# Reordering the feed-forward units that follow a two-step unit: turns, high parts and low parts

## The reference

```python
def _swiglu(x, w_gate, w_up, w_down):
    return (jax.nn.silu(x @ w_gate) * (x @ w_up)) @ w_down
```

## Time and profile before

| | us |
|---|---|
| median of the runs | 1314.61 |
| the profiled execution, its own time | 1314.64 |
| its span on the core | 1312.8 |
| PE matmul busy | 1298.3 (99%) |
| PE weight load busy | 1109.5 (85%) |
| DVE busy | 1080.2 (82%) |
| ACT busy | 791.2 (60%) |
| POOL busy | 140.0 (11%) |

### The profile page before, as it was taken

How to read it: one execution, slowest core, us unless ns; L and a number is a source line. 1 busy time by engine, 2 the same in 40 slices (tenths; PEclk the granted TensorE clock), 3 DMA queues, 4 the chain that set the end, 5 groups by cost and what they waited for, 6 DMA issues and landing times.

```text
span 1312.8 us, 19267 instructions
## 1 busy us (share of the span) xinstructions
PE 1298.3 (99%) x7299; PEld 1109.5 (85%) x7300; DVE 1080.2 (82%) x1306; ACT 791.2 (60%) x1038; POOL 140.0 (11%) x212
## 2 busy tenths in 40 slices
PE   9999999999999999999999999999999999999997
PEld 6978999998878889977888888878889988887886
DVE  6977876677999874577999979999876988999985
ACT  6674655555666645585576655666646854566661
POOL 5420000000000100183000000000000001100000
PEclk9999999999999999999999999999999999999999
DMA  9535766665698766515689868598755434779860
GB/s 318 170 107 167 241 192 192 190 206 216 204 319 271 199 222 207 188 24 193 209 257 282 271 204 299 161 326 281 201 184 181 158 100 153 285 214 310 279 183 33
DMA packets 160785, 275.53 MB, mean 210 GB/s; under 512 B 7297, under 2 KB 105874, under 8 KB 156610
## 3 DMA queue, kind: packets, MB, share of 16 engines
q1 hardware_dynamic: 150512, 226.51, 50.0%
q0 software_dynamic: 9904, 46.85, 16.0%
q10 hardware_dynamic: 290, 1.11, 0.2%
HBM read 238.24 MB, written 1.07 MB: 182 GB/s over the span
## 4 chain that ended last, share of the span: by engine, by line
PE 92%; DVE 5%; issue 2%; ACT 1%; DVEq 0%; POOL 0%; ACTq 0%
PE ps L912 18%; PE ps L914 18%; PE ps L913 18%; PE ps L734 6%; PE ps L736 6%; PE ps L735 6%; PE ps L935 3%; PE ps L936 2%; PE ps L942 2%; DVE wlo L681 2%; PE ps L3157 1%; PE ps L1922 1%; PE ps L1095 1%; PE ps L1902 1%; PE ps L1936 1%
## 5 line engine op out<-in xcount | busy, mean ns | idle before, releaser
L642 DVE TENSOR_TENSOR wlo<-raw,whi 128x1024 fp32r<-128x1024 f32 x230 | 273.7, 1224 | 45.6 <-ACT whi L632 44.4
L670 ACT ACTIVATE whi<-arena 128x2048 fp32r<-128x2048 f32 x112 | 214.6, 1916 | 98.4 <-PE ps L914 95.8
L632 ACT ACTIVATE whi<-raw 128x1024 fp32r<-128x1024 f32 x230 | 232.2, 1053 | 63.5 <-PE ps L914 45.7
L681 DVE TENSOR_TENSOR wlo<-arena,whi 128x2048 fp32r<-128x2048 f32 x112 | 255.8, 2287 | 13.8 <-ACT whi L670 12.8
L912 PE MATMUL ps<-whi,ahi 128*128 128x512 f32 x456 | 180.7, 396 | 0.0
L914 PE MATMUL ps<-wlo,ahi 128*128 128x512 f32 x456 | 177.7, 390 | 0.0
L913 PE MATMUL ps<-whi,alo 128*128 128x512 f32 x456 | 177.7, 390 | 0.0
L734 PE MATMUL ps<-ahi,whi 128*128 128x256 f32 x624 | 177.2, 284 | 0.0
L736 PE MATMUL ps<-ahi,wlo 128*128 128x256 f32 x624 | 176.6, 283 | 0.0
L735 PE MATMUL ps<-alo,whi 128*128 128x256 f32 x624 | 176.6, 283 | 0.0
L734 PEld LDWEIGHTS ps<-ahi,whi 128*128 128x128 f32 x624 | 119.7, 192 | 0.9 <-issue 0.3
(11 more groups left out here) (457 smaller groups left out, 2404.4 us busy)
## 6 DMA issues: line engine op xcount, KB each, us to landing
raw<-ffn_w_down SPq DMA_DIRECT2D x88, 512.0 KB, 10.0
arena<-ffn_w_gate SPq DMA_DIRECT2D x32, 1024.0 KB, 8.5
arena<-ffn_w_up SPq DMA_DIRECT2D x32, 1024.0 KB, 8.1
arena<-arena POOLq DMA_DIRECT2D x32, 1024.0 KB, 7.8
raw<-w_up SPq DMA_DIRECT2D x44, 512.0 KB, 4.6
raw<-ffn_w_gate SPq DMA_DIRECT2D x24, 512.0 KB, 4.7
raw<-ffn_w_up SPq DMA_DIRECT2D x24, 512.0 KB, 6.0
raw<-w_down SPq DMA_DIRECT2D x22, 512.0 KB, 4.1
```

What stands on the lines that cost most here:

```text
L632: act.activation(split_half(w_slots(slot)[0], mode), raw_half(h), ACT.Copy).then_inc(hi_ready, 1)
L642: dve.tensor_tensor(lo, raw_half(h), hi.bitcast(F32), ALU.subtract).then_inc(lo_ready, 1)
L670: act.activation(hi, src, ACT.Copy).then_inc(hi_ready, 2)
L681: dve.tensor_tensor(lo, src, hi.bitcast(F32), ALU.subtract).then_inc(lo_ready, 2)
```

## The change

In a unit behind a two-step unit:

- PE: t1 comes ahead of the turn of step 1, and the turn of step 2 comes behind b22. The order is b11, b21, t1, turn 1, t2, b22, turn 2, t3, down step 1, down step 2, t4.
- ACT: the high part of b22 and the snapshot v5 come ahead of the high part of turn 1; the high part of turn 2 comes behind the high part of t3 and the snapshot v_u2. As t1 no longer stands behind the second gated product on PE, v5 now waits for it (`gated_ready`).
- DVE: the low part of turn 1 comes behind the low part of b22, and that of turn 2 behind the low part of down step 1.

In a two-step unit that is followed by a two-step unit, also where it follows a single one, DVE writes the low part of the following t1 ahead of the second gated product.

The diff:

```diff
--- before.py
+++ after.py
@@ -1160,15 +1160,15 @@
                     product("b11", block(0, 0), z, True, True)
                     pe.wait_ge(silu_ready, done + FFN_STEPS + 2)
                     product("b21", block(0, 1), r, True, True)
+                    product("t1", block_sum(1), 1, True, True)
                     pe.wait_ge(gated_ready, done + 2)
                     turn(pair_step(before, 0), range(NT))
-                    product("t1", block_sum(1), 1, True, True)
-                    pe.wait_ge(g_ready, turns + before.steps[0] + 1)
-                    turn(pair_step(before, 1), range(NT))
                     pe.wait_ge(snap_ready, 3 * d + 1)
                     product("t2", block_sum(2), z, False, True)
                     pe.wait_ge(snap_ready, 3 * d + 2)
                     product("b22", block_sum(4), 1, False, True)
+                    pe.wait_ge(g_ready, turns + before.steps[0] + 1)
+                    turn(pair_step(before, 1), range(NT))
                     pe.wait_ge(snap_ready, 3 * d + 3)
                     product("t3", block_sum(3), z, False, True)
                 else:
@@ -1318,16 +1318,18 @@
 
                 def snap_y():
                     act.wait_ge(half_done, g.at["t1"] + 2)
+                    if before.double:
+                        act.wait_ge(gated_ready, mult_count(n) + 2 * i)
                     act.activation(v5, ps[:, 1, :], ACT.Copy).then_inc(snap_ready, 1)
 
                 if before.double:
                     act_block(act, n, c + 3)
-                    turned((0, 1), turns + before.steps[0] + 1)
                     act_block(act, n, c + 4)
                     snap_y()
-                    turned((0, 1), turns + before.steps[1] + 1, last_ghi)
+                    turned((0, 1), turns + before.steps[0] + 1)
                     act_block(act, n, c + 5)
                     snap_z()
+                    turned((0, 1), turns + before.steps[1] + 1, last_ghi)
                 else:
                     turned((0, 1), turns + before.steps[0] + 1)
                     act_block(act, n, c + 3)
@@ -1442,20 +1444,19 @@
                 g, c = parts[i], place_of(n, parts[i].at["b11"])
                 before, following, downs = parts[i - 1], parts[i + 1], len(g.downs)
                 d, z, r = g.d, ps[:, g.first, :], ps[:, 2 - g.first, :]
-                if before.double:
-                    dve_block(dve, n, c + 3)
+                if not before.double:
                     turned((0, 1), turns + before.steps[0] + 1)
-                else:
-                    turned((0, 1), turns + before.steps[0] + 1)
-                    dve_block(dve, n, c + 3)
+                dve_block(dve, n, c + 3)
                 dve.wait_ge(snap_ready, 3 * d + 1)
                 dve.wait_ge(half_done, g.at["b21"] + 2)
                 dve.tensor_tensor(g.v1, r, g.v1, ALU.add).then_inc(c_ready, 1)
                 dve_block(dve, n, c + 4)
                 if before.double:
-                    turned((0, 1), turns + before.steps[1] + 1, last_ghi, last_glo)
+                    turned((0, 1), turns + before.steps[0] + 1)
                 dve_block(dve, n, c + 5)
                 dve_block(dve, n, c + 6)
+                if before.double:
+                    turned((0, 1), turns + before.steps[1] + 1, last_ghi, last_glo)
                 dve.wait_ge(half_done, g.at["t3"] + 2)
                 dve.wait_ge(snap_ready, 3 * d + 3)
                 dve.tensor_tensor(v5, v5, z, ALU.subtract).then_inc(c_ready, 1)
@@ -1474,10 +1475,13 @@
                 dve_block(dve, n, c + 8 + downs)
                 if following.double and not before.double:
                     dve_t(dve, following, 2)
+                if following.double:
+                    dve_block(dve, n, c + 9 + downs)
                 dve.wait_ge(silu_ready, silus + 2 * i + 2)
                 dve.wait_ge(c_ready, 2 * d + 2)
                 dve.tensor_tensor(g1, g1, v5, ALU.mult).then_inc(gated_ready, 1)
-                dve_block(dve, n, c + 9 + downs)
+                if not following.double:
+                    dve_block(dve, n, c + 9 + downs)
 
             product(0, 0)
             dve.wait_ge(x_copied, 5 * f + 4)
```

## The result

The changed kernel takes 1332.2 us (median of four runs, 1331.85 to 1332.86); the kernel before took 1314.68 beside it (1314.24 to 1315.19). The ratio is 1.0132, 95% interval 1.012 to 1.0145: slower, by 17.5 us in the medians. A second set of runs gave 1332.01 against 1315.15, again 1.0132 (1.0117 to 1.0148). The forecast was 1330.2, with a range of 1323 to 1335.

The account below looks back on a forecast made before the run. PE, busy 99% of the span, bounds the kernel, with DVE near its limit. Each stage loses 0.79 us, then 1.55 in each of two loops, 3.89; four stages add 15.6 to 1314.64, giving 1330.2 us, range 1323 to 1335.

Parts of the forecast that it names:

- Part 1: Low part of t1 ahead of the second gated product on DVE: 0.15 us won once per stage, in the first unit.
- Part 2: Turn 2 behind b22: ACT's halves for down step 1 come late, PE stalls 0.94 us in each of twelve units.
- E: The end of b22 on PE, from which the forecast counts the times of later starts in a unit.
- the four terms: DVE's delay to down step 1's low parts: turn 0.63, copy 0.49, silu 0.52, first half to low part 1.09; sum 2.73.
- The cover: Before the change, down step 1's first low part was ready 1.8 us ahead of PE's need; nothing replaces that.
- Part 3: DVE's list is too full to catch up after its idle time, so the following b21 is late; 1.55 us lost per loop.
- the loop: Time from one unit to the next within a stage: 32.46 us against 30.91, the 0.94 stall included.
- The sum: Down step 1 late by 0.79, 2.34 and 3.89 us in a stage's three units; four stages 15.6 us, 1330.2 us.
- Only the down step late: Rival, chance 0.12: DVE catches up between the units, so PE stalls only at down step 1; 1325.3 us.
- The reordering hides everything: Rival, chance 0.04: the whole wait for t1 goes, 1.17 us in each stage, 4.7 us faster; 1309.9 us.
- the change does nothing: Rival, chance 0.06: t1 still waits on DVE, 0.6 us won, the down halves lose nothing; 1314.0 us.
- The clock falls: Rival, chance 0.02: PE's stalls lower its clock for one product in each of 12 units, 27 us on top; 1358 us.

Follow-up runs that it names:

- experiment 1: Changed kernel, but ACT writes the high parts of down step 1 ahead of turn 2's high part; 1314.93 us, ratio 0.9997.
- Experiment 4: Changed kernel, but ACT applies silu to v1 behind the high parts of down step 1 instead of ahead of them; 1325.28 us, ratio 1.0077.
- experiment 10: Kernel before, PE's order unchanged; only turn 2's high part on ACT and low part on DVE moved as in the changed kernel; 1315.13 us, ratio 0.9996.
- experiment 5: The changed kernel measured again, unaltered; 1332.01 us, ratio 1.0132.
- experiments 6 and 7: DVE forms the sum n2 over 64 of 2048 columns only: in the changed kernel 1322.56 us, in the kernel before 1310.4 us.
- experiment 9: Kernel of experiment 1, DVE making both gated products behind t1's low part, PE's wait for the first ahead of b11 removed; 1317.13 us, ratio 1.0013.
- experiment 7: Kernel before, with DVE's sum n2 formed over 64 of 2048 columns only; 1310.4 us, ratio 0.9965.
- experiment 8: Kernel of experiment 1, with the first gated product of each two-step unit made by POOL in place of DVE; 1316.18 us, ratio 1.0007.

## Why the prediction was right

*Part 1.* t1 was to start at 368.52; it starts at 368.53, the offset taken off. It was to win 0.15 per stage, and down step 1 of the first unit is 0.80 late, as 0.94 - 0.15 says. As a gain of its own it came out smaller: in the profile of experiment 1, where nothing else is late, the four stages win 0.06, 0.10, 0.11 and 0.09, and in the times that can't be told from nothing. The mis-sized term is the turn: its transposes take 0.35 and the product behind them 2.85 in place of 2.72 (by starts, 377.44 to 377.79 to 380.64 in the first stage of experiment 1), so it costs 0.48 and not 0.45, and 0.60 less 0.48 is 0.12; in the first stage t1 takes 0.04 longer besides.

*Part 2.* DVE at E + 2.73 came out exactly, put together from four rows of other places, and each of the four terms is there within 0.01 (0.64, 0.49, 0.52, 1.08). There are twelve waits of 0.73 to 0.74 idle, where 0.94 less 0.16 was due. Down step 1 at E + 4.11 came at E + 4.10, but here two errors met. The forecast's 0.16 for a wait of PE, taken from the wait for t1, is 0.05 until PE starts and 0.11 that the first matmuls lose behind the start. At down step 1 PE starts 0.15 behind the end of the first half's low part (381.53 + 1.23 = 382.76, and 382.90), and the loss behind the start comes on top: down step 1 lasts 5.54 (382.90 to 388.44), where it lasts 5.44 before. So the price of this wait is 0.25, and that the start itself fell on the forecast's time is luck. Experiment 4 shows that the steps of that sum act one for one, experiment 10 that the turn must be late as well. The cover that the forecast named, 1.8 us, was all the cover there was.

*Part 3.* b21 at E + 21.07 came at E + 21.05, eight times with 0.34 to 0.37 idle, and the loop is 32.51 to 32.54 where 32.46 was due. The stretch from b21 to the next turn 2 is 11.46 (399.85 to 411.31) instead of 11.39, and the difference is again the price of a wait: b21 starts 0.15 behind the end of its low part and then takes 2.80 instead of 2.72, 0.23 in all, where the forecast had 0.16. Eight loops at 0.06 more make 0.5 us.

*The sum.* The starts of down step 1 in the first stage are late by 0.80, 2.40 and 4.03, the 1.48 taken off, where 0.79, 2.34 and 3.89 were forecast. The four stages come to 16.1 us where 15.6 were forecast. The single unit behind, which was to keep 3.89, has another 0.12 in each stage (its down steps are at +5.64, those of the third unit start at +5.52), together 0.5. It does not arise there: it is what down step 1 of the third unit loses behind its own start (447.95 to 453.52, 5.57 us). In the first two units the same loss disappears in the wait for b21. So the change costs 16.6 us by the trace, and the whole 1.0 that the forecast lacks is the price of a wait of PE, 0.23 to 0.25 in place of 0.16. The span grew by 18.2; the remaining 1.5 lie ahead of 354 us and are not the change's, and in the profile of experiment 5 the same count is 16.6 of a growth of 17.0. Against the medians, 17.5 and 16.9, 0.9 and 0.3 stay unassigned.

*The rivals.* Only the down step late: wrong, there are eight waits at b21; experiments 6 and 7 show under what condition it would be right. The reordering hides everything, and the change does nothing: both wanted the halves to be covered. Experiment 1 is the kernel for which that is true, and it behaves as the second of them said; t1 goes on waiting, and experiment 9 shows for what. The clock falls: the row of the steady state has 1.00 with two stalls per unit in it.

*What remains open.* The 0.3 to 0.9 us above; and why PE starts 0.05 us behind the low part at t1 and 0.15 behind it at down step 1 and b21.

## What to carry to other kernels

When an instruction on the bound engine is moved later, look up its consumer in each of the other in-order lists and ask what stands directly behind that consumer: here 0.45 us of harmless work on PE made ACT hold back the input of the next step by 3.2 us. Recompute each cover that the move touches from the new start, by handoffs read from the same trace, and then ask whether the second-busiest engine can pay back the delay within one turn of the loop: 1.8 us of slack can't repay 3.2. Moving the consumer behind what it blocks cost nothing here (experiment 1) and is worth trying first.

## What the runs showed of the hardware

**The clock fell with PE fully busy.** The profile of the changed kernel has a stretch near 56 us, hundreds of us ahead of the changed code, where TensorE ran at its lower level, 1.2 GHz, for some of the time (granted clock 0.80 and 0.63 in these two windows):

```profile
54.00:57.00 3.00, 3.00 (x20) 2.67 (x19) 3.00 (x9) 0.00 (x0) 2.41 (x3) 0.80 0.01 3
57.00:60.00 3.00, 3.00 (x14) 2.78 (x14) 2.57 (x4) 1.10 (x3) 0.00 (x0) 0.63 0.13 31
```

The same window in the profile of experiment 5, the same kernel:

```profile
57.00:60.00 3.00, 3.00 (x19) 2.63 (x18) 3.00 (x6) 1.99 (x4) 0.00 (x0) 1.00 0.05 6
```

PE is busy for all of it in both, and 14 matmuls start where 19 did. In the slow stretch two neighbours of 128 x 256 stand 0.21 apart:

```profile
57.16 0.41 PE L736 MATMUL ps<-ahi,wlo 128*128 128x256 f32 x1
57.38 0.41 PE L734 MATMUL ps<-ahi,whi 128*128 128x256 f32 x1
```

In the kernel before they stand 0.12 apart, 0.28 long. The same matmuls are 0.06 early against the kernel before at 54 us and 1.45 late at 63 us, so it cost 1.5 us. It is in 3 of 13 profiles (the changed kernel's first, experiment 7's, and the second of experiment 1's kernel), always at this place, and PE's last idle time ahead of it is 0.2 to 0.3 us at 12.6 us. One kernel has it in one profile and not in the next, so it is not the order of the work. One thing sets the three apart: they came fastest through the program's opening. PE's first matmuls `ps<-sq,consts` start at 5.29 to 5.31 us in them and at 5.57 to 5.99 in the other ten. What links the two was not tried. It does not seem rare: these three have a mean granted clock of 0.997 over the whole execution, the other ten 0.998 or 0.999, and of the 27 runs of the kernel before beside experiment 9, the seven with 0.996 or 0.997 took 1316.17 to 1316.44 us and the other twenty 1314.36 to 1315.76. That those seven had the same stretch was not traced, and how much of the 0.3 to 0.9 us left open comes from it is not known.

**The opening differs from run to run.** By 13 us the same matmuls lie up to 1.4 us apart between profiles of kernels that are alike up to there, and that distance stays to the end. A difference of two single profiles has to be taken from a mark just ahead of the change.

**The clock held through short stalls.** In the changed kernel PE stands still 24 times for 0.3 to 0.7 us, and each window read in its stages shows 1.00, as the one above from 401 to 433 us.

**POOL and DVE together.** In experiment 8 a product of 128 x 512 in f32 took POOL 3.26 us in twelve of its sixteen cases and 2.20 in four, where DVE takes 0.69. The length goes by the DVE instruction in which it starts: each product ends 1.15 us behind the end of that instruction, be it a sum of 2.28 (2.11 of it beside POOL) or a low part of 1.22 (1.05 beside). And the DVE instruction that follows, which overlaps that last stretch, takes 1.1 us longer in all sixteen: 3.38 instead of 2.28 (L681, twelve times) and 2.31 instead of 1.22 (L642, four times). The other hundred of L681 took 2.27 to 2.29. So the two seem to have taken turns, POOL waiting for the sum and the next DVE instruction for POOL; no run varied POOL's work to test it.
